# The last head pair's pooling sums on GpSimd instead of VectorE, with head 0's query weights loaded ahead of the out projection's

## The chip, the cores and the metric

The kernel runs on one core of one Trainium2 chip, in float32. The metric is the device time of one execution in microseconds; the spread over three runs is given below. A core has TensorE (matrix products), VectorE, ScalarE and GpSimd, and SyncE (SP), which here only issues transfers.

## What is computed

Two layers of a decoder trunk over 256 tokens of width 1024. Each layer is a mixer followed by a retrieval of experts:

```
z = h @ w_in                                   # one combined projection
A = differential attention, P = causal pooling, R = gated linear recurrence (HGRN2)
x = x + gate1(c) * ((sig(gA)*A + sig(gP)*P + sig(gR)*R) @ w_out)
x = x + gate2(c) * PEER(adaLN(x))              # 8 heads, 16 of 128^2 experts each
```

The pooling is what the change touches. Group g of four has 256 channels and window w = 2, 4, 8 or 16:

```
shifted = jnp.pad(csg, ((0, 0), (w, 0), (0, 0)))[:, :S]
count = jnp.minimum(t1, w)
means.append((csg - shifted) / count[None, :, None])    # csg: running sum over time
pooled = jnp.concatenate(means, axis=-1) - p
y = einsum('bsgc,gcd->bsgd', pooled, pool_w) * pool_scale
```

The query of the retrieval is `q = h @ w_query`, 1024 columns in and 256 columns out for each head.

## The kernel before, in words

Each engine has a program of its own, written out by hand, and semaphores order them. The mixer goes over the eight heads, two at a time (a pair, and one pooling group for each pair). A loop with a register runs the first three pairs; the last pair (heads 6 and 7, group 3, window 16) is written out as `last_pair` on VectorE. TensorE is one head ahead: in the step of head 6 it makes the six projection units of head 7 (`project`, L1043, L1048, L1053), and between them head 6's scores, level products (L1090), transposed attention weights (L1101), attention (L1112 to L1114) and recurrence (L1119 to L1121). A projection unit is eight 128-row chunks. ScalarE copies each unit out of PSUM; the third unit holds the pooling channels and goes to `pb`.

VectorE's queue in the step of head 6 is, in order: `biased` (scores), `exponents`, `difference`, `decayed` (the sixteen products that the level products need, L1644 to L1647), `gates`, `pool_sums`, `turned` (a copy out of PSUM, after L1101), `assemble`, `forget` of head 7, `attended`, `recurred`, `squares`, `exponents` of head 7, `merge` of head 6, and then the steps of head 7. `pool_sums` makes the running sums by doubling, four additions with shifts of 1, 2, 4 and 8 over both heads' 272 columns, then scales and subtracts; its result `pooled` is used by `pool_out` (L1130) on TensorE, in the last step for group 3.

GpSimd's queue in this stretch is: the root of head 5's mean squares; then `qsum`, a sum over eight chunks of head 0's query weights, each scaled by a column of `acol` (L646, L649), which waits for head 3's merge and for the query weights; then the roots for heads 6 and 7 (`rsqrt`, L608 and L610). VectorE's `merge(h)` waits for the root of head h. TensorE uses `qsum` after it has finished the projections.

SP's queue, in order: the weights of head 7, rows for the conditioning vector into `braw`, the pooling weights of pair 3, `w_out` (4 MB, into the weight buffer that head 6's projection has freed), head 0's query weights (1 MB, into `braw`, once VectorE has used the last conditioning rows in it), then the bounce of `arow` and the loads that depend on later steps. `XD` holds the decays, `AH` the assembled matrix.

Of the kernel before, what the change touches and what calls it, by code (L numbers as in the profile page):

```python
# [140 lines left out]
def build(nc, x, c, ada_rows, ada_bcol, gain_col, w_in, diff_lambda, diff_subln_g, pool_w, pool_scale,  # L141
          bounds_col, hgrn_norm_g, w_out, peer_w_query, peer_sub_keys,
          peer_uv, final_g, out):
    with ExitStack() as ctx:
# [232 lines left out]
        def block_index(l, g, j, p):  # L377

            return g * sum(STEP_BLOCKS[l]) + (BLOCK0[l] + EARLY_BLOCKS[l] + STEP_BLOCKS[l][0] * j + p)
# [25 lines left out]
        def _(sp):  # L405
# [30 lines left out]
            for l in range(DEPTH):  # L436
# [88 lines left out]
                with sp.Fori(1, PAIRS - 1) as g:  # L525
                    load_pair(g, False)
                load_pair(PAIRS - 1, True)
                sp.wait_ge(s_z, UNITS * (HEADS * l + 7))
                sp.dma_start(wo_sb, w_out[l].rearrange("(k p) n -> p k n", p=P)).then_inc(s_wo, 16)
                sp.wait_ge(s_bused, 2 * block_index(l, PAIRS - 1, 0, 0))  # L530
                load_wq(l, 0, s_r[1])
                sp.wait_ge(s_rowed, l + 1)
                sp.dma_start(bounce[l], arow[0:ROWS, :]).then_inc(s_bounce, 16)
                sp.wait_ge(s_bounce, 16 * (l + 1))
# [30 lines left out]
        @block.gpsimd  # L565
        def _(pool):
            pc = Chain(pool, s_pc)

            pc(nc.gpsimd.memset(ident[:], 0.0))
            pc.sync()  # L570
            nc.gpsimd.affine_select(out=ident[:], in_=ident[:], compare_op=ALU.not_equal, fill=1.0, base=0,
                                    pattern=[[-1, P]], channel_multiplier=1).then_inc(s_id, 1)
            pc(nc.gpsimd.memset(flip[:], 0.0))
            pc(nc.gpsimd.memset(pb[:], 0.0))
            pc(nc.gpsimd.memset(mhalf[:], -0.5))
            pc(nc.gpsimd.memset(resetr[:], 1.0))
            pc(nc.gpsimd.iota(iscr[:, 0:384], pattern=[[1, 384]], base=-P, channel_multiplier=-1))
            pc(nc.gpsimd.iota(iscr[:, 384:400], pattern=[[1, 16]], base=0, channel_multiplier=0))
            pc(nc.gpsimd.memset(fm, 1.0))
            pc.sync()  # L580
            pc(nc.gpsimd.memset(resetr[:, 0:1], 0.0))
            pc(nc.gpsimd.memset(resetr[:, P:P + 1], 0.0))
            nc.gpsimd.affine_select(out=flip[:], in_=flip[:], compare_op=ALU.not_equal, fill=1.0, base=1 - P,
                                    pattern=[[1, P]], channel_multiplier=1).then_inc(s_flip, 1)

            def level_masks(c):


                sign, origin = (1, 0) if c == 0 else (-1, P - 1)
                for i in range(LEVELS):  # L590
                    m = 1 << i
                    nb = P // 2 // m
                    v = fm[:, i, c * 64:(c + 1) * 64].rearrange("p (b m) -> p b m", m=m)

                    pc.sync()
                    pc(nc.gpsimd.affine_select(out=v, in_=v, compare_op=ALU.is_ge, fill=0.0, base=origin,
                                               pattern=[[-2 * m, nb], [0, m]], channel_multiplier=sign))
                    pc.sync()
                    last = nc.gpsimd.affine_select(out=v, in_=v, compare_op=ALU.is_ge, fill=0.0, base=m - 1 - origin,
                                                   pattern=[[2 * m, nb], [0, m]], channel_multiplier=-sign)  # L600
                    if i < LEVELS - 1 or c == 0:
                        pc(last)
                return last

            def root(n, width, c):

                apart(pool)
                pc(nc.gpsimd.tensor_scalar(rsb[:, c:c + n], ms[:, c:c + n], 1.0 / width, EPS, ALU.mult, ALU.add))  # L608
                pc.sync()
                return nc.gpsimd.tensor_tensor(rs[:, c:c + n], rsb[:, c:c + n], mhalf[:, 0:n], ALU.pow)  # L610

            def rsqrt(k, n, width, c=0):

                pool.wait_ge(s_ms, k + 1)
                root(n, width, c).then_inc(s_rs, 1)

            pool.wait_ge(s_square0, 1)
            rsqrt(0, NT, D)
            level_masks(0)
            level_masks(1).then_inc(s_const, 1)  # L620
            pool.wait_ge(s_cstv, 1)
            for a in (0, 256):
                n = 256 if a == 0 else 128
                off = 0 if a == 0 else 128
                nc.gpsimd.affine_select(out=nd[:, a:a + n], in_=nd[:, a:a + n], compare_op=ALU.is_ge, fill=MASKED,
                                        base=P - off, pattern=[[-1, n]], channel_multiplier=1).then_inc(s_const, 1)

            NR = HEADS + 3
            for l in range(DEPTH):
                if l:  # L630
                    rsqrt(NR * l, 1, D, 1)
                start = pc.n
                with pool.Fori(0, PAIRS - 1) as g:
                    pc.base, pc.n = g * 2 + start, 0
                    for j in range(2):
                        rsqrt(g * 2 + j + (NR * l + 1), 4, P)
                assert pc.n == 2
                pc.base, pc.n = 0, start + (PAIRS - 1) * pc.n


                pool.wait_ge(s_mix, mixed(l) + 4)
                pool.wait_ge(s_r[1], 16 * (l + 1))
                apart(pool)
                for k in range(KC):
                    term = lamr[:] if k else qsum[:]
                    pc(nc.gpsimd.tensor_scalar(term, wqv[0][:, k, :], acol[:, KC + k:KC + k + 1], None, ALU.mult, ALU.bypass))  # L646
                    pc.sync()
                    if k:
                        i = nc.gpsimd.tensor_tensor(qsum[:], qsum[:], lamr[:], ALU.add)  # L649
                        if k < KC - 1:  # L650
                            pc(i)
                            pc.sync()
                i.then_inc(s_qsum, 1)
                for h in range(HEADS - 2, HEADS):
                    rsqrt(h + (NR * l + 1), 4, P)
                pool.wait_ge(s_left_ms, l + 1)
                pool.wait_ge(s_ms, NR * l + HEADS + 2)
                apart(pool)
                pc(nc.gpsimd.tensor_scalar(rsb[:, 0:1], ms[:, 1:2], ms[:, 0:1], EPS, ALU.add, ALU.add))
                pc.sync()  # L660
                nc.gpsimd.tensor_tensor(rs[:, 0:1], rsb[:, 0:1], mhalf[:, 0:1], ALU.pow).then_inc(s_rs, 1)


                for g in range(LGROUPS):
                    if g == NBUF + 4:
                        rsqrt(NR * l + HEADS + 2, 1, D, 1)
                    i, q, b = g // GROUPS, g % GROUPS, g % NBUF
                    if g == LEAD + NBUF + 1 and l + 1 < DEPTH:
                        pool.wait_ge(s_lead_ms, l + 1)
                        root(1, D, 0).then_inc(s_lead_rs, 1)  # L670
                    elif g == LEAD + NBUF + 1:
                        pool.wait_ge(s_early_ms, 1)
                        root(1, D, 0).then_inc(s_early_rs, 1)
                    if g == 0:
                        pool.wait_ge(s_top, l + 1)
                    elif q == 0 or g == EARLY // GROUP:
                        pool.wait_ge(s_route, 2 * HEADS * l + i + 1)
                    if g >= NBUF:
                        pool.wait_ge(s_vacc, summed(l) + g - NBUF + 1)
                    elif SLOT0[b] < 4:  # L680
                        pool.wait_ge(s_wod, 4 * (l + 1))
                    apart(pool)
                    for s in range(GROUP):
                        k = q * GROUP + s
                        if g == 0 and s == 1:
                            pool.wait_ge(s_best, l + 1)
                            apart(pool)
                        nc.gpsimd.indirect_dma_start(  # L688
                            out=pair_rows[b][s], out_offset=None, in_=uv_rows,
                            in_offset=bass.IndirectOffsetOnAxis(ap=idx[i % 2][:, k:k + 1], axis=0)).then_inc(s_uv[b], 16)  # L690

            pool.wait_ge(s_parts, 1)
            pool.wait_ge(s_square, 1)
            apart(pool)
            pc(nc.gpsimd.tensor_scalar(rsb[:, 1:2], ms[:, 3:4], ms[:, 2:3], EPS, ALU.add, ALU.add))
            pc.sync()
            nc.gpsimd.tensor_tensor(rs[:, 1:2], rsb[:, 1:2], mhalf[:, 0:1], ALU.pow).then_inc(s_rs, 1)
# [643 lines left out]
        def _(dve):  # L1341
# [117 lines left out]
            for l in range(DEPTH):  # L1459
# [294 lines left out]
                def last_pair(h, g):  # L1754
# [3 lines left out]
                    difference(h)  # L1758
                    decayed(h, 0)
                    gates(h, 0, g)  # L1760
                    pool_sums(h + 1, g)
                    turned(h)
                    assemble(h)
                    forget(h + 1, 1)
# [332 lines left out]
```

## Time and profile before

| | us |
|---|---|
| runs before, median of 3 (lowest to highest) | 2106.34 (2103.97 to 2112.12) |
| the profiled execution | 2106.78 |
| its span, first to last instruction | 2105.0 |
| TensorE busy | 1866.1 |
| VectorE busy | 1480.1 |
| ScalarE busy | 693.7 |
| GpSimd busy | 639.9 |

Times in the rows are microseconds from the start of the span, unless marked ns. A row of a timeline gives start, duration, engine, source line, operation, output and inputs with their shapes, the number of instructions merged in it, and in brackets the idle time ahead of it with what ended it. PE is TensorE, DVE VectorE, ACT ScalarE, POOL GpSimd, SPq the queue of SP. The last step of the head loop (head 6) lies at about 325 to 373 us in layer 0 and at 1361 to 1410 us in layer 1. L1352, L1349 and L1346 are helpers that many places of VectorE's program share.

### The profile page before, as it was taken

Reading aid. Unit: us, or ns where it says so; the run is one execution under the profiler, and the core shown is the slowest. Engines: PE = TensorE matmul, PEld = TensorE weight load, DVE = VectorE, ACT = ScalarE, POOL = GpSimd, SP = SyncE. Lnnn points to the kernel's source line nnn. Section 1 sums busy time; section 2 is a strip of 40 time slices with the busy share of each in tenths; the row PEclk is TensorE's granted clock in tenths of the full one; section 3 lists DMA queues with packets and bytes.
Section 4 is the critical chain, followed back from the end, with each engine's and each line's share of the span. In section 5 each row is a group of like instructions: output and inputs, shape, how many; then the busy total and the mean of one; then the engine's idle time right before and its main releaser. Section 6 shows DMA issues by size and latency. Waiting matters only on the chain.

```text
span 2105.0 us, 22605 instructions
## 1 busy us (share of the span) xinstructions
PE 1866.1 (89%) x6632; PEld 1094.3 (52%) x6632; DVE 1480.1 (70%) x4045; ACT 693.7 (33%) x1939; POOL 639.9 (30%) x638
## 2 busy tenths in 40 slices
PE   6999999988888888888799999998888888888877
PEld 5677777644434434333377777775443443443432
DVE  5777777787667667667537676687866766767774
ACT  2223323243333333333323322232433333333332
POOL 4000003244444444444300000033444444344442
PEclk9999999999999999999999999999999999999999
DMA  9757553699999999999986554348999999999997
GB/s 389 285 190 279 206 208 128 239 426 426 427 425 427 421 424 425 426 415 417 392 314 254 189 182 158 137 165 314 424 427 427 426 421 424 426 415 426 425 409 292
DMA packets 118053, 717.39 MB, mean 341 GB/s; under 512 B 13040, under 2 KB 17456, under 8 KB 50096
## 3 DMA queue, kind: packets, MB, share of 16 engines
q0 software_dynamic: 73728, 536.90, 61.0%
q1 hardware_dynamic: 44208, 179.20, 22.5%
q8 instruction: 40, 0.66, 0.1%
q14 instruction: 77, 0.63, 0.1%
HBM read 714.97 MB, written 1.08 MB: 340 GB/s over the span
## 4 chain that ended last, share of the span: by engine, by line
PE 47%; DMA 21%; DVE 21%; issue 4%; ACT 3%; SPq 2%; POOL 2%; DVEq 0%; POOLq 0%; ACTq 0%
DMA wall<-in_peer_uv,idx 19%; PE PS L1298 17%; PE PS L1043 9%; DVE wall L1355 7%; PE PS L1048 7%; PE PS L1053 5%; PE PS L1063 2%; POOL wall L688 2%; DMA braw<-in_ada_rows 2%; DVE pos L1849 1%; DVE ts L1846 1%; ACT M L904 1%; DVE M L1946 1%; DVE M L1949 1%; DVE M L1951 1%
## 5 line engine op out<-in xcount | busy, mean ns | idle before, releaser
L1298 PE MATMUL PS<-wall,M 128*128 128x512 f32 x2032 | 955.5, 619 | 203.1 <-ACT M L904 200.4
L1355 DVE CUSTOM_DVE_ANT_0 wall<-wall,tok 128x1024 f32<-128x1024 f32 x512 | 606.7, 1223 | 333.8 <-DMA wall<-in_peer_uv,idx 333.7
L688 POOL DMA_INDIRECT wall<-in_peer_uv,idx x512 | 554.6, 1083 | 713.6 <-PE PS L1298 561.0
L1298 PEld LDWEIGHTS PS<-wall,M 128*128 128x128 f32 x2032 | 383.7, 197 | 729.8 <-issue 413.8
L890 ACT ACTIVATE dg<-dg 128x2 f32<-128x2 f32 x254 | 51.7, 204 | 746.6 <-DVE dg L1355 746.6
L1043 PE MATMUL PS<-hT,wall 128*128 128x256 f32 x1120 | 247.8, 380 | 0.0
L1043 PEld LDWEIGHTS PS<-hT,wall 128*128 128x128 f32 x1120 | 211.6, 190 | 29.9
L1048 PE MATMUL PS<-wall,hT 128*128 128x512 f32 x480 | 210.8, 592 | 0.2 <-ACT M L757 0.2
L608 POOL TENSOR_SCALAR rsb<-ms 128x4 f32<-128x4 f32 (+2 forms) x22 | 4.7, 212 | 643.5 <-DVE ms L1355 643.3
L904 ACT ACTIVATE M<-turn,wgt 128x128 f32<-128x128 f32 x508 | 176.1, 394 | 24.6 <-ACT wgt L897 1.5
L1048 PEld LDWEIGHTS PS<-wall,hT 128*128 128x128 f32 x480 | 90.0, 190 | 102.0 <-issue 101.3
L897 ACT ACTIVATE wgt<-dg,gate 128x1 f32<-128x1 f32 x508 | 121.9, 286 | 10.3
L1355 DVE CUSTOM_DVE_ANT_0 braw<-braw,crow 128x1024 f32<-128x1024 f32 x78 | 93.0, 1221 | 35.7 <-DMA braw<-in_ada_rows 35.6
L1053 PE MATMUL PS<-wall,hT 128*128 128x256 f32 x480 | 107.7, 383 | 0.0
L1053 PEld LDWEIGHTS PS<-wall,hT 128*128 128x128 f32 x480 | 91.8, 193 | 12.9 <-issue 0.5
L765 ACT ACTIVATE M<-PS 128x256 f32<-128x256 f32 x32 | 12.3, 383 | 211.6 <-PE PS L1048 209.6
L1352 DVE SCALAR_TENSOR_TENSOR mix<-nd,slopes,PS 128x384 f32<-128x384 f32 x32 | 18.2, 611 | 62.6 <-PE PS L1073 62.3
L1063 PE MATMUL PS<-wall,hT 128*128 128x512 f32 x128 | 57.5, 597 | 2.2 <-ACT hT L721 2.2
L1242 PEld LDWEIGHTS PS<-hT,mix 128*128 128x128 f32 x384 | 44.8, 192 | 5.7 <-issue 5.7
L1666 DVE COPY_PREDICATED mix<-lmask,PS 128x128 f32<-128x128 uint8 x112 | 37.9, 338 | 11.5
L788 ACT ACTIVATE ring<-ring 128x2048 f32<-128x2048 f32 x16 | 30.6, 1912 | 45.6 <-DVE ring L1622 45.6
L1242 PE MATMUL PS<-hT,mix 128*128 128x128 f32 x384 | 44.8, 275 | 0.0
(294 smaller groups left out, 1878.4 us busy)
## 6 DMA issues: line engine op xcount, KB each, us to landing
wall<-in_w_in SPq DMA_DIRECT2D x120, 704.0 KB, 10.2
braw<-in_ada_rows SPq DMA_DIRECT2D x76, 512.0 KB, 4.3
wall<-in_w_out SPq DMA_DIRECT2D x2, 4096.0 KB, 15.3
wall<-in_peer_uv,idx POOLq DMA_INDIRECT x512
wall<-in_ada_rows SPq DMA_DIRECT2D x6, 1024.0 KB, 12.5
mix<-in_peer_w_query SPq DMA_DIRECT2D x6, 1024.0 KB, 4.9
ada<-out SPq DMA_DIRECT2D x2, 2048.0 KB, 6.9
wall<-in_peer_w_query SPq DMA_DIRECT2D x4, 1024.0 KB, 5.6
```

What stands on the lines that cost most here:

```text
L688: nc.gpsimd.indirect_dma_start(out=pair_rows[b][s], out_offset=None, in_=uv_rows, in_offset=bass.IndirectOffsetOnAxis(ap=idx[i % 2][:, k:k ...
L890: nc.scalar.activation(gel[b], dots[b], ACT.Gelu).then_inc(s_gel, 1)
L897: i = nc.scalar.activation(wgt[:, b, s:s + 1], gel[b][:, s:s + 1], ACT.Copy, scale=gate[tile % NT][:, k:k + 1])
L904: i = nc.scalar.activation(diag[:, b, s, :], ident[:], ACT.Copy, scale=wgt[:, b, s:s + 1])
L1043: ins = mm(b[:, i * T:(i + 1) * T], wz[j][:, k, s, :], hT[:, k, :], start=(k == 0), stop=(k == KC - 1))
L1048: ins = mm(b, hT[:, k, t * P:(t + 1) * P], wz[j][:, k, HI:ZP + 1, :], start=(k == 0), stop=(k == KC - 1))
L1053: ins = mm(b[:, t * 256:(t + 1) * 256], hT[:, k, t * P:(t + 1) * P], wz[j][:, k, AV:ZR + 1:ZR - AV, :], start=(k == 0), stop=(k == KC - 1))
L1063: i = mm(bank(B_WO[t][hf]), hT[:, k, t * P:(t + 1) * P], wo_sb[:, k, hf * 512:(hf + 1) * 512], start=(k == 0), stop=(k == KC - 1))
L1242: i = mm(dst[:, a * P:(a + 1) * P], wqv[h][:, k, a * P:(a + 1) * P], hT[:, k, t * P:(t + 1) * P], start=(k == 0 and a == 0), stop=(k == KC ...
L1298: ins = mm(bank(B_ACC + 2 * t + hf), diag[:, b, s, :], pair_rows[b][s][:, D + hf * 512:D + (hf + 1) * 512], start=(i == FIRST_TILE[t] and ...
L1355: return v.tensor_tensor_reduce(out=o, in0=a, in1=b, scale=1.0, scalar=0.0, op0=ALU.mult, op1=ALU.add, accum_out=acc)
L1666: i = v.copy_predicated(out=lview(ah2.rearrange("p c t -> p (c t)"), lv)[:, :, 1, :], mask=lmask[:, lv, :].rearrange("p (b m) -> p b m", m=m),
```

## The change

Two edits, in both layers. The sums of the last pair are taken out of VectorE's `last_pair` and written out for GpSimd, behind `qsum` and ahead of the roots for heads 6 and 7. The mask `pm`, which is one everywhere for group 3, is dropped, and the scaling and the subtraction are separate instructions there: seven in all. And SP issues head 0's query weights ahead of `w_out`.

```
                 load_pair(PAIRS - 1, True)
+                sp.wait_ge(s_bused, 2 * block_index(l, PAIRS - 1, 0, 0))
+                load_wq(l, 0, s_r[1])
                 sp.wait_ge(s_z, UNITS * (HEADS * l + 7))
                 sp.dma_start(wo_sb, w_out[l].rearrange("(k p) n -> p k n", p=P)).then_inc(s_wo, 16)
-                sp.wait_ge(s_bused, 2 * block_index(l, PAIRS - 1, 0, 0))
-                load_wq(l, 0, s_r[1])
                 sp.wait_ge(s_rowed, l + 1)
...
                 i.then_inc(s_qsum, 1)
+                g = PAIRS - 1
+                pool.wait_ge(s_pooled, PAIRS * l + g)
+                pool.wait_ge(s_y, PAIRS * l + g)
+                pool.wait_ge(s_zev, UNITS * (HEADS * l + HEADS - 1) + 3)
+                apart(pool)
+                src = pb[:]
+                for k in range(4):
+                    d, lo = 1 << k, (2 << k) - 1
+                    dst = pt[k % 2]
+                    pc(nc.gpsimd.tensor_tensor(dst[:, :, lo:PW], src[:, :, lo - d:PW - d], src[:, :, lo:PW], ALU.add))
+                    pc.sync()
+                    src = dst
+                pc(nc.gpsimd.tensor_scalar(pooled[:, :, 16:T], src[:, :, 32:PW], 1.0 / WINDOWS[g], None, ALU.mult, ALU.bypass))
+                pc(nc.gpsimd.tensor_tensor(pooled[:, :, 0:16], src[:, :, 16:32], rc16[:, g:g + 1, :].to_broadcast([P, 2, 16]), ALU.mult))
+                pc.sync()
+                nc.gpsimd.tensor_tensor(pooled[:], pooled[:], pb[:, :, 16:PW], ALU.subtract).then_inc(s_pooled, 1)
                 for h in range(HEADS - 2, HEADS):
                     rsqrt(h + (NR * l + 1), 4, P)
...
                     gates(h, 0, g)
-                    pool_sums(h + 1, g)
                     turned(h)
```

## Rows read from the trace of the kernel before

**Rows 1.** The page's head: the span and its instructions.

```profile
span 2105.0 us, 22605 instructions
```

**Rows 2.** Windows: length, busy PE, PEld, DVE, ACT, POOL, clock, DMA share, GB/s.

```profile
325.00:373.00 48.00, 48.00 (x214) 36.12 (x214) 38.20 (x120) 16.18 (x30) 17.74 (x18) 1.00 0.41 150
1361.00:1410.00 49.00, 49.00 (x219) 37.01 (x219) 36.60 (x116) 16.51 (x30) 16.95 (x18) 1.00 0.41 153
```

**Rows 3.** The chain that ended last, layer 0: start, duration, what.

```profile
354.43 1.56 PE PS L1090 x14
...
356.99 6.87 PE PS L1048 x16
...
365.73 6.91 PE PS L1053 x32
...
380.90 1.56 PE PS L1090 x14
```

**Rows 4.** Timeline of VectorE, layer 0.

```profile
337.07 1.14 DVE L1352 SCALAR_TENSOR_TENSOR mix<-nd,slopes,PS 128x384 f32<-128x384 f32 x2 [5.81 <-PE PS L1073]
...
346.07 0.29 DVE L1644 TENSOR_TENSOR ring<-ring,M 128x128 f32<-128x128 f32 x1 [0.39 <-ACT ring L788]
...
349.14 0.29 DVE L1647 TENSOR_TENSOR ring<-ring,mix 128x128 f32<-128x128 f32 x1
...
351.42 1.00 DVE L1352 SCALAR_TENSOR_TENSOR wall<-pb,pm 128x542 f32<-128x542 f32 x1
...
356.83 0.66 DVE L1588 TENSOR_TENSOR wall<-wall,pb 128x32 f32<-128x32 f32 x1
...
372.15 0.61 DVE L1352 SCALAR_TENSOR_TENSOR tok<-mix,rs 128x128 f32<-128x128 f32 x2
...
379.15 0.28 DVE L1647 TENSOR_TENSOR ring<-ring,mix 128x128 f32<-128x128 f32 x1
```

**Rows 5.** Timeline of GpSimd, layer 0.

```profile
348.26 4.05 POOL L646 TENSOR_SCALAR mix<-braw,acol 128x256 f32<-128x256 f32 x2 [22.78 <-DMA braw<-in_peer_w_query]
...
363.42 0.92 POOL L646 TENSOR_SCALAR mix<-braw,acol 128x256 f32<-128x256 f32 x1
364.43 0.72 POOL L649 TENSOR_TENSOR mix<-mix 128x256 f32<-128x256 f32 x1
367.75 0.22 POOL L608 TENSOR_SCALAR rsb<-ms 128x4 f32<-128x4 f32 x1 [2.60 <-DVE ms L1355]
368.06 1.42 POOL L610 TENSOR_TENSOR rs<-rsb,mhalf 128x4 f32<-128x4 f32 x1
```

**Rows 6.** SP's queue in layer 0, then loads by line with median us to landing.

```profile
329.62 0.43 SPq L529 DMA_DIRECT2D wall<-in_w_out  x1
330.98 0.33 SPq L420 DMA_DIRECT2D braw<-in_peer_w_query  x1
...
mix<-in_peer_w_query SPq DMA_DIRECT2D x6, 1024.0 KB, 4.9
```

**Rows 7.** Timeline of VectorE, layer 1.

```profile
1373.74 1.14 DVE L1352 SCALAR_TENSOR_TENSOR mix<-nd,slopes,PS 128x384 f32<-128x384 f32 x2 [8.64 <-PE PS L1073]
...
1382.74 0.30 DVE L1644 TENSOR_TENSOR ring<-ring,M 128x128 f32<-128x128 f32 x1 [0.39 <-ACT ring L788]
...
1386.75 0.28 DVE L1647 TENSOR_TENSOR ring<-ring,mix 128x128 f32<-128x128 f32 x1
...
1389.64 0.77 DVE L1352 SCALAR_TENSOR_TENSOR wall<-pb,pm 128x542 f32<-128x542 f32 x1
...
1394.71 0.66 DVE L1588 TENSOR_TENSOR wall<-wall,pb 128x32 f32<-128x32 f32 x1
...
1408.82 0.60 DVE L1352 SCALAR_TENSOR_TENSOR tok<-mix,rs 128x128 f32<-128x128 f32 x2
```

**Rows 8.** Layer 1: SP's queue, then the chain that ended last.

```profile
1366.65 0.58 SPq L420 DMA_DIRECT2D braw<-in_peer_w_query  x1
...
1391.11 1.56 PE PS L1090 x14
```

## The prediction

> **What bounds the kernel now.** I read the page first: it gives the span, 2105.0 us [rows 1], and the table above gives TensorE busy in 1866.1 of it, 89%. An average over stages says nothing about one stage, so the second view is the table of windows over the last step of the head loop, once in each layer, because both edits act there. TensorE is busy in 48.00 of 48.00 us and in 49.00 of 49.00 us, at full granted clock, while VectorE is busy in 38.20 and 36.60 us [rows 2]. The third view is the chain that ended last. Through this stretch it runs on TensorE without a piece of another engine: head 6's level products, head 7's fourth and fifth projection units, and head 6's attention products follow each other [rows 3]. Only behind the projections does VectorE enter the chain. The timelines of VectorE and GpSimd then give the slack of each wait [rows 4, 5]. The question of this prediction is whether anything in TensorE's queue waits for what the change shortens or delays.
>
> **Part 1, VectorE loses head pair 3's sums.** It now makes them from 351.42 to 357.49 us (the last row starts at 356.83 and takes 0.66) [rows 4], 6.07 us, and in layer 1 from 1389.64 to 1395.37, 5.73 us [rows 7]. If VectorE were what the end waits for, this would give 11.8 us. Next in its queue stands the copy of head 6's turned weights, which needs TensorE's transposes. They stand ahead of the fourth projection unit, which starts at 356.99 [rows 3]. So VectorE would stand still for some 5 us and then start the copy about 0.5 us earlier. Its result, the assembled matrix, is wanted only after that unit of 6.87 us, at 363.9, and TensorE shows no wait there [rows 2]. In layer 1 the transposes should end as long after the first level product as in layer 0, 2.56 us, so at 1393.67 [rows 3, 8]; at most 1.7 us of the 5.7 could be used by the copy, and again the fourth unit covers it. I cost the removal at 0 in both layers. The cover is TensorE's projection queue; without it the price would be a gain of up to 5.9 us a layer.
>
> **Part 2, the query weights move ahead of the out projection's.** In layer 0 they are issued at 330.98, behind the 4 MB issued at 329.62, and GpSimd gets them only at 348.26 [rows 5, 6]. The same 1 MB load into other buffers lands 4.9 us (median) after its issue [rows 6], hence at about 336 to 337; I take 336.5. In layer 1 they are issued at 1366.65 [rows 8]; I take that plus 4.9 and 1.5 more for the pooling scales just ahead: 1373. The w_out load moves from 329.62 to behind 330.98 + 0.33, 1.7 us later, in layer 0 and by the length of one issue in layer 1. Its data then end where both loads together end now, plus that shift: 350 in layer 0. The first out-projection matmul stands behind the fifth unit, which ends at 372.6 [rows 3], so 22 us cover it. Price 0. The later loads of the SP queue (the bounce of arow, ada, the other query weights) wait for things behind this point, so they don't move.
>
> **Part 3, GpSimd's work.** It now makes the eight-chunk sum (qsum) in 348.26 to 365.15, 16.9 us [rows 5]. Undisturbed, a product takes 0.92 and an addition 0.72 us with 0.1 between them: 8 x 0.92 + 7 x 0.72 + 1.4 = 13.8. It was stretched by 1.22. Then come the seven new instructions, which no row shows in this size. Four additions over 542, 538, 530 and 514 elements, one scaling of 480, one product of 32, one subtraction of 512. Lower bound, if size cost nothing: 6 x 0.72 + 0.92 + 0.6 = 5.8 us. Upper bound, all in proportion to size from 0.72 and 0.92 for 256 [rows 5]: 2124 and 512 elements at 2.81 ns are 7.4, the scaling 1.7, the small one 0.7, gaps 0.6: 10.4 us. Taking 0.2 us as the part that doesn't grow (a 128x4 scaling from 367.75 takes 0.22 [rows 5]) gives 8.8, which I take, nearer to the upper end because the sizes are twice that of the row. Times 1.22: 10.7 us.
>
> Layer 0: 336.5 + 16.9 + 10.7 = 364.1. Layer 1: 1373 + 16.9 + 10.7 = 1400.6. The input, head 7's third unit in pb, is there: VectorE reads it without a wait at 351.42 and 1389.64 [rows 4, 7], and qsum ends later. The pooled result is wanted only in the last step's pool products, 20 us later. What is queued behind it matters more: the root of head 6's squares, and behind that head 7's root. Head 6's root takes 1.73 us (367.75 to 369.48) [rows 5] and VectorE asks for it at 372.15 [rows 4] and 1408.82 [rows 7]. So the sums may end at 370.4 and 1407.1 at no cost, and a further 1.4 us is free, since head 7's products for the levels end at 379.44 [rows 4] and TensorE takes them at 380.90 [rows 3]. The margins are 7.7 us and 7.9 us. Price 0.
>
> **Part 4, contention.** The sum qsum now falls on head 6's scores, exponents and decays on VectorE, whose end TensorE needs for the level products. In layer 0 the sixteen products of the decays ran from 346.07 to 349.43, 3.36 us, mostly alone; the one GpSimd product that began beside them, at 348.26, belongs to a row that took 4.05 us for two [rows 4, 5]. In layer 1 the same sixteen ran beside qsum from 1382.74 to 1387.03, 4.29 us [rows 7], a stretch of 1.28. So both engines suffer. Applied to the whole of head 6's VectorE work ahead of the level products (337.07 to 349.43, 12.36 us), it ends at 352.9 instead of 349.4, and TensorE asks at 354.43 [rows 3]; in layer 1 at 1373.74 + 15.8 = 1389.5, and TensorE asks at 1391.11 [rows 8]. Both still fit, by 1.5 us. The low bound is no stretch. Price 0.
>
> The Trainium skill (SBUF — State Buffer, "Who interferes with whom") says that a VectorE instruction with two SBUF inputs and a GpSimd instruction that reads SBUF exclude each other, the later one waiting for the whole of the earlier. Taken at its worst it would stop VectorE for the whole of GpSimd's 12 us beside this work. The trace agrees only in part: under a running qsum the decays of layer 1 lost 0.9 us, not most of their time. I give the strict form a chance of its own, as the second rival.
>
> **The sum.** 0 + 0 + 0 + 0. The profiled execution took 2106.78 us beside a span of 2105.0; the median of the runs is 2106.34, so I predict 2106.3.
>
> **Rivals.**
> First, GpSimd is late and holds head 6's root. Against it stand 7.7 us of margin and the idle time on VectorE that the change itself opens. For it: the first two products took 4.05 us instead of 1.94, a stretch of 2.1 [rows 5]. If 1.8, most of the way from 1.22 to that, held throughout, 1.8 x (13.8 + 10.4) = 43.6 us would end the sums at 380.1 and 1416.6, the roots at 381.8 and 1418.3. Past 372.15 + 1.4 and 1408.82 + 1.4 that is 8.3 and 8.1 us of loss: 2122.7. It decides from a mean stretch near 1.5 (35.3 us after the landing).
>
> Second, VectorE is held by GpSimd so that the decays come late and TensorE waits. It decides from a stretch of 1.40 (17.3 us from 337.07 to 354.43). If VectorE stood still for all 12 us of GpSimd work, the decays would end at 361.4 and 1398.1, and TensorE would lose 7 us in each layer: 2120.3. The 1.28 of layer 1 speaks against it. The Trainium skill's rule above is this case.
>
> Third, on the other side, faster: VectorE's freed time reaches the end after all, through something in its queue that starts earlier and that I read as covered. All of it would give 2106.3 - 11.8 = 2094.5, half 2100.4. Against it is TensorE without an idle microsecond in both windows [rows 2].
>
> Fourth, the load doesn't come early, since both loads share the engines instead of following each other. Then qsum starts about 3 us later than I said, which the margins hold: no change.
>
> **Numbers.** Forecast, with the fourth case: 0.88. First rival 0.05, second 0.04, third 0.03. The measurement tells 0.5% (10.5 us) at best; the three runs themselves spread over 8 us. Only the full form of a rival passes that, so same has 0.88 and the smaller forms of the rivals fall in it too. Faster 0.04, slower 0.08. The range for 8 in 10 is the likeliest case with the spread of the runs and small forms of the rivals on either side: 2100 (half of the third) to 2113 (about 3.5 us lost in each layer).
>
> **What the new profile should show.** Query weights landing near 336.5 and 1373, qsum beginning there, seven GpSimd instructions ending near 364 and 1401. VectorE idle some 4 to 5 us ahead of the copy of the turned weights. TensorE again busy throughout 325 to 373 and 1361 to 1410. Head 6's root ready before VectorE asks. I am wrong if a wait for the decays shows ahead of the level products, or a wait for the root ahead of head 6's merge, or if the step of head 7 starts earlier than now.

## The result, and the profile after

The changed kernel is slower by a little: a median of 2111.64 us (2108.72 to 2113.86, 8 runs) beside 2104.88 us for the kernel before in the same comparison; ratio 1.0026, 95% interval 1.0015 to 1.0036, so 3 to 8 us. The profiled execution took 2111.43 us, with a span of 2109.6 us, 4.6 us more than before. The time lies inside the range, and inside what the prediction called no change (0.5%), but the interval excludes zero: there is a loss, and it has a cause.

The first view is the table of windows over the last step of the head loop (length, busy PE, PEld, DVE, ACT, POOL, clock, DMA share, GB/s), as [rows 2]. The windows start 1 and 2 us later, because this execution entered the step later (in layer 0 it was 1.5 us late already at 326 us, ahead of anything that the change touches), and end 5 us later, so that the whole waits lie inside.

```profile
326.00:378.00 52.00, 49.49 (x223) 37.03 (x223) 40.61 (x114) 16.91 (x30) 24.66 (x25) 1.00 0.40 150
1363.00:1415.00 52.00, 49.70 (x222) 37.30 (x222) 37.49 (x110) 16.41 (x30) 24.96 (x26) 1.00 0.39 143
```

TensorE, without an idle moment in [rows 2], now stands still for 2.51 and 2.30 us. Its timeline says where, in layer 0 and then in layer 1:

```profile
348.89 7.03 PE L1066 MATMUL PS<-wall,hT 128*128 128x512 f32 x16
358.43 1.83 PE L1108 MATMUL PS<-ring 128*128 128x128 f32 x14 [2.51 <-DVE ring L1665]
...
1386.61 7.03 PE L1066 MATMUL PS<-wall,hT 128*128 128x512 f32 x16
1395.94 1.83 PE L1108 MATMUL PS<-ring 128*128 128x128 f32 x14 [2.30 <-DVE ring L1665]
```

L1108 is head 6's level products, L1665 the last of the sixteen decay products. The two waits add up to 4.8 us, which lies inside the 3 to 8 us of the loss. VectorE's timeline in layer 0 shows why that product is late (it answers to [rows 4]):

```profile
338.56 1.14 DVE L1370 SCALAR_TENSOR_TENSOR mix<-nd,slopes,PS 128x384 f32<-128x384 f32 x2 [5.79 <-PE PS L1091]
...
342.19 0.77 DVE L1364 COPY mix<-mix 128x128 f32<-128x128 f32 x1
...
350.03 0.29 DVE L1662 TENSOR_TENSOR ring<-ring,M 128x128 f32<-128x128 f32 x1
350.25 0.84 DVE L1663 TENSOR_TENSOR ring<-ring,mix 128x128 f32<-128x128 f32 x1
351.01 0.28 DVE L1662 TENSOR_TENSOR ring<-ring,M 128x128 f32<-128x128 f32 x1
...
351.41 0.48 DVE L1662 TENSOR_TENSOR ring<-ring,M 128x128 f32<-128x128 f32 x1
...
353.15 1.17 DVE L1663 TENSOR_TENSOR ring<-ring,mix 128x128 f32<-128x128 f32 x1
354.25 0.28 DVE L1662 TENSOR_TENSOR ring<-ring,M 128x128 f32<-128x128 f32 x1
354.45 1.17 DVE L1663 TENSOR_TENSOR ring<-ring,mix 128x128 f32<-128x128 f32 x1
355.54 0.28 DVE L1662 TENSOR_TENSOR ring<-ring,M 128x128 f32<-128x128 f32 x1
355.74 1.16 DVE L1663 TENSOR_TENSOR ring<-ring,mix 128x128 f32<-128x128 f32 x1
356.82 0.28 DVE L1664 TENSOR_TENSOR ring<-ring,M 128x128 f32<-128x128 f32 x1
357.02 1.35 DVE L1665 TENSOR_TENSOR ring<-ring,mix 128x128 f32<-128x128 f32 x1
```

And GpSimd's timeline beside it, as [rows 5]:

```profile
338.01 1.97 POOL L646 TENSOR_SCALAR mix<-braw,acol 128x256 f32<-128x256 f32 x2 [11.03 <-DMA braw<-in_peer_w_query]
...
351.00 1.19 POOL L646 TENSOR_SCALAR mix<-braw,acol 128x256 f32<-128x256 f32 x1
352.28 0.80 POOL L649 TENSOR_TENSOR mix<-mix 128x256 f32<-128x256 f32 x1
353.04 1.14 POOL L665 TENSOR_TENSOR wall<-pb 128x542 f32<-128x542 f32 x1
354.26 3.97 POOL L665 TENSOR_TENSOR wall<-wall 128x538 f32<-128x538 f32 x3
358.32 1.66 POOL L668 TENSOR_SCALAR wall<-wall 128x480 f32<-128x480 f32 x1
360.06 0.28 POOL L669 TENSOR_TENSOR wall<-wall,rc 128x32 f32<-128x32 f32 x1
360.42 1.40 POOL L671 TENSOR_TENSOR wall<-wall,pb 128x512 f32<-128x512 f32 x1
372.02 0.22 POOL L608 TENSOR_SCALAR rsb<-ms 128x4 f32<-128x4 f32 x1 [10.20 <-DVE ms L1373]
```

From 353.04 on, two products get through for each addition: one of 0.28 us and one that takes 1.16 to 1.35 us, although its work is the same. Head 6's work on VectorE up to the last decay product takes 358.37 - 338.56 = 19.81 us instead of 12.36, 7.45 more. Up to the start of the tenth decay product (353.15, and 347.92 in the kernel before) it lost 353.15 - 338.56 - (347.92 - 337.07) = 3.74 us, beside qsum; the last seven lost the other 3.71, beside the additions. The margin was 354.43 - 349.43 = 5.0 us. Either loss alone fits into it; both together pass it by 2.45 us, and TensorE waits 2.51. In layer 1 the same work takes 19.60 us and the wait is 2.30.

### The profile page after: what moved, and what is told of

Same layout as the page of the kernel before. It is cut to its first block, busy times and chain, and to the rows that moved or that the text cites. A ratio compares the mean times of both kernels' runs of the same rounds, so it can differ in the third digit from the quotient of the medians.

```text
span 2109.6 us, 22609 instructions
## 1 busy us (share of the span) xinstructions
PE 1871.6 (89%) x6632; PEld 1096.3 (52%) x6632; DVE 1483.5 (70%) x4031; ACT 693.7 (33%) x1939; POOL 656.8 (31%) x652
## 4 chain that ended last, share of the span: by engine, by line
PE 46%; DMA 21%; DVE 21%; issue 4%; POOL 3%; ACT 3%; SPq 2%; DVEq 0%; POOLq 0%; ACTq 0%
DMA wall<-in_peer_uv,idx 20%; PE PS L1316 15%; PE PS L1061 9%; PE PS L1066 8%; DVE wall L1373 7%; PE PS L1071 5%; POOL wall L706 3%; PE PS L1081 2%; DVE pos L1866 1%; DVE ts L1863 1%; ACT M L922 1%; PE PS L1108 1%; DVE M L1966 1%; DVE M L1963 1%; DVE M L1968 1%
## 5 line engine op out<-in xcount | busy, mean ns | idle before, releaser
L1316 PE MATMUL PS<-wall,M 128*128 128x512 f32 x2032 | 959.6, 622 | 197.5 <-ACT M L922 196.9
```

The costliest lines, as they stand in the source:

```text
L1316: ins = mm(bank(B_ACC + 2 * t + hf), diag[:, b, s, :], pair_rows[b][s][:, D + hf * 512:D + (hf + 1) * 512], start=(i == FIRST_TILE[t] and ...
```

## The experiments

A is the theory that VectorE is held (an instruction of it stands still until GpSimd's has read) while GpSimd's additions read, and that this, with the additions falling on the last decay products, is the whole loss. The rivals are given with each run. The first four runs were compared with a median before of 2105.12 us, the last four with one of 2106.32.

**Each half of the change alone.** The first kernel only swaps the loads; the second only moves the sums.

```
 load order only:   + sp.wait_ge(s_bused, ...); load_wq(l, 0, s_r[1])   # ahead of w_out
                      pool_sums stays in last_pair on VectorE
 sums only:           w_out, then the query weights, as before; the sums on GpSimd
```

> Only the order of the two loads is changed; the sums stay on VectorE. The theory that GpSimd's long two-input additions hold VectorE (A) expects no measurable loss: the sum over the query weights still falls on head 6's work on VectorE, which ends some 4 us later than before, near 353 to 354 us, but TensorE asks for the decays only near 354.5 to 356, so a wait of at most 0.3 us a layer; ratio to before 0.999 to 1.001. The rival (B), that the earlier GpSimd sum and the load itself cost the time, expects the waits of about 2 us a layer to stay and a ratio near 1.0025.

Measured: 2105.64 us, ratio 1.0004 (0.9995 to 1.0013). TensorE has no idle in either window. qsum runs over the same work of VectorE, and the first and last rows of that work are:

```profile
337.49 1.14 DVE L1352 SCALAR_TENSOR_TENSOR mix<-nd,slopes,PS 128x384 f32<-128x384 f32 x2 [5.80 <-PE PS L1073]
...
353.20 0.28 DVE L1647 TENSOR_TENSOR ring<-ring,mix 128x128 f32<-128x128 f32 x1
```

That is 15.99 us, a stretch of 1.29, where the prediction had 1.28. TensorE took the products at 354.69, 1.2 us later. The load order and the earlier qsum cost nothing by themselves, but they use up 3.6 of the 5 us of margin. The rival B falls. The sums on VectorE took from 355.33 to 359.59 here, 4.26 us, where they took 6.07 in the kernel before with qsum beside them: part of what the change takes off VectorE is time in which it was being held.

> Only the sums are moved to GpSimd; the loads keep their old order. Then the sum over the query weights ends near 365 and the additions fall on 365 to 375 us, beside the exponents of head 7. A expects no wait ahead of head 6's level products, but the root of head 6 late by 3 to 6 us (asked for at 372), VectorE's exponents of head 7 stretched by 1 to 3 us, and TensorE waiting 2 to 5 us a layer in the last step: ratio 1.002 to 1.005. A theory (B) that blames the load order expects a ratio of 1.000.

Measured: 2113.47 us, ratio 1.0047 (1.0035 to 1.006), the slowest of all. No wait ahead of the level products, as A says. The additions (364.96 to 369.89) fall on head 6's squares, and the subtraction behind them on head 7's exponents. VectorE, then GpSimd's subtraction:

```profile
367.58 1.11 DVE L1373 CUSTOM_DVE_ANT_0 mix<-mix 128x128 f32<-128x128 f32 x1
...
368.73 1.31 DVE L1373 CUSTOM_DVE_ANT_0 mix<-mix 128x128 f32<-128x128 f32 x1
...
371.96 2.58 DVE L1631 TENSOR_TENSOR ring<-mix 128x128 f32<-128x128 f32 x7
```

```profile
371.91 1.27 POOL L671 TENSOR_TENSOR wall<-wall,pb 128x512 f32<-128x512 f32 x1
```

The two engines behind them, ScalarE and TensorE, then TensorE's window behind its wait (columns as in [rows 2]):

```profile
378.30 1.06 ACT L739 ACTIVATE hT<-PS 128x512 f32<-128x512 f32 x2
```

```profile
379.42 7.11 PE L1081 MATMUL PS<-wall,hT 128*128 128x512 f32 x12 [3.46 <-ACT hT L739]
```

```profile
379.40:383.00 3.60, 3.58 (x6) 1.69 (x7) 3.56 (x17) 2.92 (x12) 0.00 (x0) 0.68 0.05 16
```

A square took 0.29 us before, here up to 1.31; the seven products of 371.96 took 1.50 before, here 2.58. The exponents come late, ScalarE makes head 7's decays before it copies hT, and TensorE waits 3.46 us for that copy (2.51 in layer 1), where it waited 0.40 in the kernel before. In layer 0 the wait has a second price: behind it the granted clock was 0.68 of full speed (a mean over a stretch that lay partly at 1.2 and partly at 2.4 GHz), and the same twelve products took 7.11 us instead of 5.42. Behind the waits of 2.51 us here and of 2.51 and 2.30 us in the changed kernel it stayed at 1.00. So 5.2 us of added waits and 1.7 us of clock are shown, of 8.4 us between the medians. The size was expected, the path only in part: I had the root of head 6 as the late thing, but it was ready at 374.83 and VectorE itself reached its merge only at 376.37. So the moved load does help: without it the sums cost more (8.4 us instead of 6.8, and the two intervals, 1.0035 to 1.006 and 1.0015 to 1.0036, hardly touch).

**The place of the additions.** The changed kernel with one wait more on GpSimd, ahead of the sums:

```
                 pool.wait_ge(s_zev, UNITS * (HEADS * l + HEADS - 1) + 3)
+                pool.wait_ge(s_X, HEADS * l + HEADS - 1)     # head 6's decay products are done
```

> The changed kernel with one more wait: GpSimd begins the pooling sums only after VectorE has finished head 6's sixteen decay products. A expects the waits of 2.5 and 2.3 us ahead of head 6's level products to fall to 0 to 0.3 us, the sums to end near 364 and without a wait for head 6's root, and the time to come back to that of before, ratio 0.999 to 1.001. If the loss had another source (the rest of the step shifted, run to run spread), the waits would go and the ratio stay near 1.0025.

Measured: 2105.54 us, ratio 1.0002 (0.9992 to 1.0013). No wait ahead of the level products in either layer. The additions now stand beside the gates and VectorE's idle stretch:

```profile
355.64 1.70 POOL L666 TENSOR_TENSOR wall<-pb 128x542 f32<-128x542 f32 x1 [1.82 <-DVE ring L1666]
357.42 3.71 POOL L666 TENSOR_TENSOR wall<-wall 128x538 f32<-128x538 f32 x3
```

Letting them wait 1.82 us takes the waits away, and the loss with them. This run shows the cause: the same instructions on the same engine, and only what they lie beside differs.

**The length of the additions.** Each cut in two, one for each head's columns.

```
-  tensor_tensor(dst[:, :, lo:PW], src[:, :, lo - d:PW - d], src[:, :, lo:PW], ALU.add)
+  for h in range(2):
+      tensor_tensor(dst[:, h, lo:PW], src[:, h, lo - d:PW - d], src[:, h, lo:PW], ALU.add)
```

> The changed kernel with each of the four additions cut in two, one for each head's 271 columns: eight additions of about 0.65 us instead of four of about 1.2. If GpSimd holds VectorE for whole instructions and VectorE gets two products through between them (A), twice as many gaps let twice as many through: the products of the decays end about 2 us earlier and TensorE's waits fall from 2.5 and 2.3 to 0 to 0.8 us a layer. If the two engines only share a rate (C), the length of the instructions does not matter, and the waits stay at 2 us or more.

Measured: 2106.95 us, ratio 1.001 (1.0002 to 1.0019). The waits are 0.8 and 1.5 us: at the upper end of what A expected in layer 0, above it in layer 1, and below the 2 us of C in both. They add up to 2.3 us, and the medians are 1.8 us apart, so the time goes down with the waits. The held products are shorter:

```profile
353.25 0.72 DVE L1664 TENSOR_TENSOR ring<-ring,mix 128x128 f32<-128x128 f32 x1
353.90 0.72 DVE L1663 TENSOR_TENSOR ring<-ring,M 128x128 f32<-128x128 f32 x1
354.54 0.28 DVE L1664 TENSOR_TENSOR ring<-ring,mix 128x128 f32<-128x128 f32 x1
```

0.72 us is 0.44 over 0.28, where the whole additions gave 0.89 over it. The hold is half as long for half as many elements, and the last seven products lose 2.2 us (356.94 - 353.25, less the 1.51 of the kernel before) instead of 3.7.

**What in an addition holds VectorE.** Two kernels in which GpSimd does something else in the same place. They leave out the last group's running sums, so they answer only the question of the hold and are no replacement for the changed kernel.

```
-  tensor_tensor(dst[:, :, lo:PW], src[:, :, lo - d:PW - d], src[:, :, lo:PW], ALU.add)
 fills:      + for h in range(2): memset(dst[:, :, 0:PW], float(h))
 one input:  + tensor_scalar(dst[:, :, lo:PW], src[:, :, lo:PW], 1.0, None, ALU.mult, ALU.bypass)
```

> The changed kernel, but GpSimd fills the scratch of the running sums instead of adding: each of the four additions is replaced by two fills of 544 elements, about 0.54 us each (the last group's pooling is left out of the computation). The place and the time on GpSimd stay about the same, 4 x 1.2 us, but nothing reads SBUF. If the hold comes from GpSimd's reads (A), the seven decay products beside the fills keep their 0.2 us pace, the waits of 2.5 and 2.3 us ahead of the level products go to 0, ratio 0.999 to 1.001. If any GpSimd instruction holds VectorE, or the wait has to do with the place of the sums in GpSimd's queue, the waits stay above 1.5 us.

Measured: 2103.97 us, ratio 0.9992 (0.998 to 1.0003); no wait ahead of the level products. Eight fills keep GpSimd busy for 5.0 us, and VectorE's products beside them keep their pace:

```profile
350.84 5.00 POOL L666 MEMSET wall<- 128x544 f32 x8
```

```profile
351.17 0.28 DVE L1664 TENSOR_TENSOR ring<-ring,M 128x128 f32<-128x128 f32 x1
```

> The changed kernel with each addition replaced by a scaling by one of the same 542 to 514 elements (one input instead of two; the last group's running sums are left out of the computation), estimated from 0.92 us for 256 elements at 1.4 to 1.9 us each. If one read is enough to hold VectorE for the whole instruction (A), VectorE loses as much per instruction as the instruction is long, and TensorE's waits are 2.5 to 4 us a layer, ratio 1.0025 to 1.004. If only two-input instructions hold it, the waits go to 0.

Measured: 2104.4 us, ratio 0.999 (0.9978 to 1.0002), no wait ahead of the level products. A's part that the hold is as long as the instruction is wrong. GpSimd's instructions are longer than the additions, and VectorE loses less:

```profile
352.27 1.61 POOL L665 TENSOR_SCALAR wall<-pb 128x542 f32<-128x542 f32 x1
353.97 5.22 POOL L665 TENSOR_SCALAR wall<-wall 128x538 f32<-128x538 f32 x3
```

```profile
352.36 0.72 DVE L1663 TENSOR_TENSOR ring<-ring,mix 128x128 f32<-128x128 f32 x1
353.00 0.28 DVE L1662 TENSOR_TENSOR ring<-ring,M 128x128 f32<-128x128 f32 x1
...
354.21 0.85 DVE L1561 TENSOR_TENSOR mix<-M,mix 128x256 f32<-128x256 f32 x1
```

In 1.61 us only one product is held, by 0.44 us; the next hold, again 0.44 over the usual 0.41, comes with the next instruction. The waits went to 0, as the alternative written for this run forecast, but its reason (only two-input instructions hold) is wrong too: one input holds for half as long as two, and that is short enough for the margin.

**A move where the chain does run over VectorE.** The kernel before, with head 7's gains taken from behind the squares into the gap ahead of its turned weights (the load that waited for them waits for the squares instead):

```
                     attend_gate(1)
+                    ch(recur_gate(1))
+                    gates_ready(h + 1, 6)
+                    recur_gains(1).then_inc(s_gated, 1)
                     turned(h + 1)
...
                     squares()
-                    gates_ready(h + 1, 6)
-                    recur_gains(1).then_inc(s_gated, 1)
```

> The kernel before with another move on VectorE: head 7's gains of the recurrence (three products, 1.2 us) go from behind its squares, where the chain runs over VectorE, to the 1.8 us in which VectorE waits for head 7's turned weights. The theory that work counts only where the chain runs over its engine expects 0.8 to 1.2 us less a layer, 1.6 to 2.4 us in all, ratio near 0.999, more than the 6 us a layer that the change took off VectorE gave. The rival: another wait takes its place (the root of head 7, the pool products) and the ratio is 1.000.

Measured: 2105.02 us, ratio 0.9993 (0.9981 to 1.0006): not told apart from no change. The gap took the products (VectorE's wait there fell from 1.81 to 0.49 us), but a wait for head 7's root took their place, 0.57 us, and VectorE's result came only 0.3 us sooner after the recurrence (5.10 instead of 5.37 us). TensorE did not use even that: from the recurrence (L1119) to the second group of out-projection products it needs 393.43 - 387.72 = 5.71 us before and 393.95 - 388.24 = 5.71 us here.

```profile
388.24 0.49 PE L1119 MATMUL PS<-M,mix 128*128 128x128 f32 x2 [0.49 <-DVE mix L1666]
...
393.31 0.42 PE L1059 MATMUL PS<-turn,tok 128*128 128x128 f32 x2
393.95 3.70 PE L1063 MATMUL PS<-wall,hT 128*128 128x512 f32 x8 [0.22 <-ACT hT L842]
```

Its own queue reaches the transposes (L1059) 5.07 us after the recurrence in both kernels, and behind them it now waits for ScalarE's copy. The expected 0.8 to 1.2 us a layer were not there; the chain through VectorE had a second one, over TensorE and ScalarE, close behind.

> The sums on GpSimd behind the decay products (as in the gated run) together with the gains moved early. Expected: no wait ahead of the level products, and the 1.6 to 2.4 us of the gains; ratio 0.9985 to 1.0, the same as the gains alone on the kernel before, since the place of the sums is covered either way.

Measured: 2104.11 us, ratio 0.9989 (0.9978 to 1.0). The interval touches 1, so this is not shown to beat the kernel before, and TensorE's timeline has the same 5.71 us. No version was found that clearly beats both.

## Why the prediction was wrong

**The bound and part 1 held.** TensorE's queue sets this stretch, and 6 us a layer taken off VectorE gave nothing. In the gated run, where TensorE waits for no decay, the ratio is 1.0002. The sign that I had named, VectorE idle for 4 to 5 us ahead of the copy of the turned weights, did not show: it was idle for 0.61 us in each layer, since its work ahead of that point had grown by 7.45 us.

**Part 2 held.** The query weights were issued at 332.48 and GpSimd had them at 338.01; relative to the start of head 6's scores that is 0.55 us ahead, forecast 0.57.

**Part 3, durations.** The seven instructions took from 353.04 to 361.82, 8.8 us, the undisturbed value of the estimate; the stretch of 1.22 was not there, nor was qsum's (15.1 us, forecast 16.9). Measured from head 6's scores, the sums ended 23.3 us on instead of 27.0. In these contests VectorE lost more than I had assumed and GpSimd less. Head 6's root was never late, so the first rival did not happen.

**Part 4 is the step that failed.** Its stretch of 1.28 for VectorE beside qsum was right (1.29 in the load-only run). But it was the price beside qsum alone; the additions were put at nothing, without a reason. By my own numbers the decays ended at 352.9 and the additions began at 353.4, and in layer 1 at 1389.5 and 1389.9. That would have kept them apart by 0.4 to 0.5 us, which is inside the error of both estimates, and I never compared the two. qsum ended 1.8 us sooner than forecast, the additions began 14.5 us after the start of head 6's scores where the decays need 16.0 even without them (the load-only run), and once they overlapped, each addition let only two products through, which kept the rest of the decays beside further additions. The result is a stretch of 1.60, past the 1.40 at which the second rival decides. That rival happened, at about a third of its price: 2.5 and 2.3 us instead of 7 and 7. VectorE lost 7.45 us and not 12, since it was held only for part of GpSimd's time, and 5.0 us of either figure are covered by the margin. Its chance of 0.04 was too low. The 1.5 us of margin that spoke against it came from a sum that omitted one of the two loads on VectorE. That the time still fell into the range is no merit of the mechanism: the range had room for small forms of the rivals, and this was one.

**The Trainium skill's rule** (SBUF — State Buffer, "Who interferes with whom"): the runs agree with it that two-input VectorE instructions contend with GpSimd instructions that read SBUF and not with those that only write (fills: no hold). The same page (section "SBUF: two separate sides") says that the one that starts first keeps the port "for the whole instruction". The runs don't agree with that: an instruction of 1.61 us held VectorE by 0.44 us.

Of the 6.8 us between the medians, 4.8 are shown as waits. The rest, 2 us, lies inside the interval (3 to 8 us); TensorE's waits for the decay products grew from nothing to 4.8 us over the whole kernel, while its largest other wait (for ScalarE, 200.4 us before and 196.9 after) moved by 3.5 us the other way. Whether the rest is more than spread stays open.

## What to carry to other kernels

Work moved to GpSimd has a place as well as a length: look at what VectorE does beside it, and whether TensorE waits for that. Where two estimated times decide whether two things overlap, price the overlap if they are within the error of each other, or write the order as a wait: one semaphore wait was worth the whole loss here. And taking time off an engine pays only where no other engine's queue covers the same stretch; the chain names one cover, and a second may lie close behind it (0.3 us in the run with the gains moved).

## What the runs showed of the hardware

The hold on a two-input VectorE instruction went with the elements that the GpSimd instruction reads, not with how long it takes: two inputs of 542 held it 0.89 us (1.17 instead of 0.28), two of 271 held it 0.44, one of 542 held it 0.44 (in an instruction of 1.61 us), one of 256 held it 0.20 (0.48 instead of 0.28, beside qsum's scalings), and a fill held it 0. That is about 0.8 ns for each element read by a partition (0.89 us for 1084). It is a rule of thumb from a few cases: the two inputs of 256 in qsum come out dearer, 0.53 to 0.56 us, the last addition (two inputs of 514) held its product for 1.07 us, in the sums-only run a square was held for up to 1.02 us (1.31 instead of 0.29), and in the gated run two products of 128x256 for 0.78 and 0.76 us. Why these differ was not tested. GpSimd's two-input additions of 538 elements took 1.3 us each, so VectorE lost two thirds of that time, against a third of it beside qsum (0.20 + 0.53 in the 2.04 us from 351.00 to 353.04), whose scalings read one input.

Not only two-input instructions of VectorE were held: beside an addition of qsum a 128x128 copy took 0.77 us (342.19) instead of 0.23, 0.54 more. No run was made to separate the kinds.
